# Where the eight sample rows get their scan projections and their convolution

## What is computed

```python
h = rmsnorm(x, norm_mix_w)
q, k, v, z, xbc, dt_raw = split_in(h @ w_in)      # 1024 | 256 | 256 | 1024 | 1536 | 16 columns
o_att = sink_attention(q, cache_k + k, cache_v + v, ...)
xpad = concat([state_conv, xbc], axis=1)          # 3 old rows, 1 new
new_conv = xpad[:, -3:]
xbc = silu(causal_dwconv(xpad, conv_w) + conv_b)  # 4 taps, 1536 channels
dt = softplus(dt_raw + dt_bias)
y, new_ssm = ssd_recurrent(xs, dt, A, bs, cs, ssm)
x += concat(rmsnorm(o_att), rmsnorm((y + d_skip * xs) * silu(z))) @ w_out
```

## Time and profile before

| | |
|---|---|
| time, median of 3 runs | 4440.74 us (4435.55 to 4442.08) |
| time of the profiled execution | 4443.82 us |
| its span in the trace | 4442.0 us |
| PE busy | 3836.0 us, 86% of the span |
| VectorE busy | 2496.3 us, 56% |
| ScalarE busy | 1308.7 us, 29% |
| GpSimd busy | 1353.9 us, 30% |

### The profile page before, as it was taken

How to read it: one execution, slowest core, us unless ns; L and a number is a source line. 1 busy time by engine, 2 the same in 40 slices (tenths; PEclk the granted TensorE clock), 3 DMA queues, 4 the chain that set the end, 5 groups by cost and what they waited for, 6 DMA issues and landing times.

```text
span 4442.0 us, 41911 instructions
## 1 busy us (share of the span) xinstructions
PE 3836.0 (86%) x11597; PEld 1976.8 (45%) x11597; DVE 2496.3 (56%) x5472; ACT 1308.7 (29%) x3879; POOL 1353.9 (30%) x1243
## 2 busy tenths in 40 slices
PE   8998789896888699998889999889999888877776
PEld 4555244553452345543445543345554344433332
DVE  2333256653412577654577754587755468766664
ACT  2333023331010132342233342233324233333332
POOL 0000033330000233443433434433344333334443
PEclk9997799997897899999999999999999999999999
DMA  6000000003604599999999999999999999999997
GB/s 211 29 28 33 33 15 19 19 9 122 266 15 165 231 418 418 419 418 421 420 402 405 418 420 420 421 394 410 412 420 412 421 419 400 418 418 397 419 421 298
DMA packets 227231, 1316.62 MB, mean 296 GB/s; under 512 B 27225, under 2 KB 43518, under 8 KB 93345
## 3 DMA queue, kind: packets, MB, share of 16 engines
q0 software_dynamic: 148608, 1082.20, 58.9%
q1 hardware_dynamic: 77272, 232.15, 14.0%
q10 hardware_dynamic: 1152, 0.00, 0.0%
HBM read 1283.65 MB, written 32.68 MB: 296 GB/s over the span
## 4 chain that ended last, share of the span: by engine, by line
DMA 26%; PE 26%; DVE 7%; issue 3%; ACT 2%; DVEq 1%; ACTq 0%; POOL 0%; POOLq 0%
DMA ex_ring<-in_expert_uv,ex_idx 25%; PE psum L2758 17%; DVE ex_ring L3143 4%; PE psum L2787 4%; PE psum L2736 3%; ACT ex_diag L2939 1%; PE psum L2806 1%; PE psum L2831 0%; ACT ex_weight L2934 0%; DMA ex_ring<-in_expert_uv,ex_idxT 0%; PE psum L2848 0%; POOL ex_ring L2678 0%; DMA pair_p<-scratch_mixed 0%; DVE ex_top_at L3038 0%; ACT ex_dots L2930 0%
## 5 line engine op out<-in xcount | busy, mean ns | idle before, releaser
L2758 PE MATMUL psum<-ex_ring,ex_diag 128*128 128x512 f32 x4096 | 1919.8, 613 | 332.1 <-ACT ex_diag L2939 308.9
L3143 DVE CUSTOM_DVE_ANT_0 ex_ring<-ex_ring,ex_x_rows 128x1024 f32<-128x1024 f32 x1024 | 1250.4, 1226 | 825.1 <-DMA ex_ring<-in_expert_uv,ex_idx 752.6
L2678 POOL DMA_INDIRECT ex_ring<-in_expert_uv,ex_idx x1024 | 1137.1, 1110 | 1754.8 <-PE psum L2758 1556.4
L2758 PEld LDWEIGHTS psum<-ex_ring,ex_diag 128*128 128x128 f32 x4096 | 772.6, 195 | 1303.1 <-issue 850.9
L2930 ACT ACTIVATE ex_dots<-ex_dots 128x2 f32<-128x2 f32 x512 | 104.1, 203 | 1790.5 <-DVEq L3146 1790.0
L2939 ACT ACTIVATE ex_diag<-ident,ex_weight 128x128 f32<-128x128 f32 x1024 | 355.0, 394 | 36.9 <-issue 1.7
L1062 PE MATMUL psum<-w_zx,ssd_hT 128*128 128x512 f32 (+1 forms) x768 | 295.8, 542 | 21.5 <-DMA ssd_hT<-scratch_hT 20.8
L2736 PE MATMUL psum<-ex_xT,ex_chunk 128*128 128x256 f32 (+1 forms) x1280 | 278.2, 362 | 4.2 <-ACT ex_sub L2915 2.9
L2736 PEld LDWEIGHTS psum<-ex_xT,ex_chunk 128*128 128x128 f32 x1280 | 230.3, 192 | 98.3 <-issue 77.4
L2934 ACT ACTIVATE ex_weight<-ex_gates,ex_dots 128x1 f32<-128x1 f32 x1024 | 245.8, 287 | 36.2 <-issue 1.1
L1062 PEld LDWEIGHTS psum<-w_zx,ssd_hT 128*128 128x128 f32 x768 | 137.6, 193 | 176.3 <-issue 154.6
(11 more groups left out here) (455 smaller groups left out, 3708.6 us busy)
## 6 DMA issues: line engine op xcount, KB each, us to landing
ex_chunk<-in_route_wq SPq DMA_DIRECT2D x80, 512.0 KB, 7.9
ex_chunk<-in_w_out SPq DMA_DIRECT2D x48, 512.0 KB, 9.5
ex_ring<-in_expert_uv,ex_idx POOLq DMA_INDIRECT x1024, 20.3
ex_chunk<-in_read_wq SPq DMA_DIRECT2D x24, 512.0 KB, 8.0
ex_chunk<-in_w_mo SPq DMA_DIRECT2D x24, 512.0 KB, 7.9
w_zx<-in_w_in SPq DMA_DIRECT2D x1, 10304.0 KB, 35.6
w_out<-in_w_out SPq DMA_DIRECT2D x2, 4096.0 KB
w_out<-in_cache_mem_k SPq DMA_DIRECT2D x8, 1024.0 KB, 13.3
```

Source lines behind the costliest of these rows:

```text
L2678: nc.gpsimd.indirect_dma_start(out=ring[:, n % RING, :], out_offset=None, in_=io["expert_uv"], in_offset=bass.IndirectOffsetOnAxis(ap=idx[ ...
L2758: ins = nc.tensor.matmul(psum[c][:], diag[:, q % 3, s, :], ring[:, n % RING, D + c * BANK:D + (c + 1) * BANK], start=(n % SLOTS == 0), sto ...
L3143: nc.vector.tensor_tensor_reduce(ring[:, n % RING, 0:D], ring[:, n % RING, 0:D], x_rows[:, tile % 3, :], 1.0, 0.0, ALU.mult, ALU.add, dots ...
```

## The change

The stage `ssd_sample_inputs` is gone. Its projections stand in `attention_sample`: the first of the six blocks behind the scores and ahead of the turning of p, the five others behind the value products. ScalarE takes all six blocks from PSUM into a buffer `own_zx` that lives until the scan's end: two takes behind its exponentials, four behind the square of `o`; z's two blocks with SiLU. The value products go to other PSUM banks, and the norm of `o` gets a buffer of its own. The convolution, softplus and their loads and stores stand in `ssd_prompt`: VectorE runs `own_step` ahead of its first turn, ScalarE its three activations ahead of its first turn (and so ahead of the first `load_rstd`), SyncE its loads and stores between those of the head. The products of the taps are made in place, in the buffers of the weights.

```diff
-def attention_sample(nc, io, psum, shared, w_qkv):
+def attention_sample(nc, io, psum, shared, w_qkv, w_zx, own_zx):
...
+        zx_chunks = ((1024, 4), (1536, 6), (2048, 7), (2560, 0), (0, 4), (512, 6))
+        value_banks = (1, 2, 3, 5)
...
         def _(pe):
+            def project_zx(i):
+                cols, bank = zx_cols(i), zx_chunks[i][1]
+                if i >= 4:
+                    pe.wait_ge(zx_taken, i - 3)
+                for b in range(DB):
+                    ins = nc.tensor.matmul(psum[bank][0:DEC, 0:cols.stop - cols.start], hT[:, b, :], w_zx[:, b, cols],
+                                           start=(b == 0), stop=(b == DB - 1))
+                ins.then_inc(zx_projected, 1)
...
             ins.then_inc(scored, 1)
+            project_zx(0)
             pe.wait_ge(p_ready, 1)
...
             ins.then_inc(valued, 1)
+            for i in range(1, 6):
+                project_zx(i)
...
         def _(act):
+            def take_zx(i):
+                cols, bank = zx_cols(i), zx_chunks[i][1]
+                act.wait_ge(zx_projected, i + 1)
+                nc.scalar.activation(own_zx[:, cols], psum[bank][0:DEC, 0:cols.stop - cols.start],
+                                     ACT.Silu if i >= 4 else ACT.Copy, scale=rstd[:]).then_inc(zx_taken, 1)
...
             nc.scalar.activation(esink[:], esink[:], ACT.Exp).then_inc(esum, 1)
+            take_zx(0)
+            take_zx(1)
             act.wait_ge(o_in, 16)
             nc.scalar.activation(junk[:], o[:], ACT.Square, accum_out=ms[:]).then_inc(oms_ready, 1)
+            for i in range(2, 6):
+                take_zx(i)
+            act.wait_ge(zx_taken, 6)
...
-def ssd_prompt(nc, io, psum, shared, w_zx):
+def ssd_prompt(nc, io, psum, shared, w_zx, own_zx):
...
             sp.dma_start(skip[:], io["d_skip"].broadcast_to([P, NH])).then_inc(loaded, 16)
+            sp.dma_start(past[:], io["state_conv"]).then_inc(own_loaded, 16)
+            for k in range(CONV - 1):
+                sp.dma_start(weights[:, k, :], io["conv_w"][k:k + 1, :].broadcast_to([DEC, CONV_DIM])).then_inc(own_loaded, 16)
+            sp.dma_start(io["s_conv"][:, 0:CONV - 2, :], io["state_conv"][:, 1:CONV - 1, :]).then_inc(own_stored, 16)
+            sp.dma_start(io["s_conv"][:, CONV - 2, :], own_x).then_inc(own_stored, 16)
+            sp.dma_start(io["gates"], own_zx[:, 0:D]).then_inc(own_stored, 16)
+            sp.wait_ge(own_weighed, 1)
+            sp.dma_start(last_weight, io["conv_w"][CONV - 1:CONV, :].broadcast_to([DEC, CONV_DIM])).then_inc(own_last_in, 16)
+            sp.dma_start(own_bias, io["conv_b"].broadcast_to([DEC, CONV_DIM])).then_inc(own_last_in, 16)
             load(1)
+            sp.wait_ge(own_dt_ready, 1)
+            sp.dma_start(io["dts"], own_raw[:]).then_inc(own_stored, 16)
+            sp.wait_ge(own_cv_ready, 1)
+            sp.dma_start(io["rows2"], cv_own[:, 0:D]).then_inc(own_stored, 16)
+            sp.dma_start(io["bcs"], cv_own[:, D:CONV_DIM]).then_inc(own_stored, 16)
             with sp.Fori(0, TILES - 2) as t:
...
             nc.scalar.activation(rate[:], rate[:], ACT.Exp).then_inc(rates_ready, 1)
+            act.wait_ge(own_neg_ready, 1)
+            nc.scalar.activation(own_e[:], own_neg[:], ACT.Exp).then_inc(own_e_ready, 1)
+            act.wait_ge(own_u_ready, 1)
+            nc.scalar.activation(own_neg[:], own_u[:], ACT.Ln).then_inc(own_log_ready, 1)
+            act.wait_ge(own_convolved, 1)
+            nc.scalar.activation(cv_own, cv_own, ACT.Silu).then_inc(own_cv_ready, 1)
             turn(None, 0)
...
+            def own_step():
+                nc.vector.tensor_tensor(own_raw[:], own_dt, dt_bias[0:DEC, :], ALU.add)
+                dve.drain()
+                nc.vector.scalar_tensor_tensor(own_neg[:], own_raw[:], -1.0, own_raw[:], ALU.mult, ALU.min)
+                nc.vector.tensor_scalar(own_raw[:], own_raw[:], 0.0, None, ALU.max)
+                dve.drain()
+                dve.sem_inc(own_neg_ready, 1)
+                dve.wait_ge(own_loaded, 16 * CONV)
+                for k in range(CONV - 1):
+                    nc.vector.tensor_tensor(weights[:, k, :], weights[:, k, :], past[:, k, :], ALU.mult)
+                dve.drain()
+                dve.sem_inc(own_weighed, 1)
+                dve.wait_ge(own_e_ready, 1)
+                nc.vector.tensor_scalar(own_u[:], own_e[:], 1.0, None, ALU.add).then_inc(own_u_ready, 1)
+                nc.vector.tensor_tensor(cv_own, cv_own, weights[:, 1, :], ALU.add)
...
+                nc.vector.tensor_tensor(cv_own, cv_own, weights[:, 2, :], ALU.add)
...
+                dve.wait_ge(own_last_in, 32)
+                nc.vector.tensor_tensor(last_weight, last_weight, own_x, ALU.mult)
+                dve.drain()
+                nc.vector.tensor_tensor(cv_own, cv_own, last_weight, ALU.add)
+                dve.wait_ge(own_log_ready, 1)
+                nc.vector.tensor_tensor(own_raw[:], own_raw[:], own_neg[:], ALU.add).then_inc(own_dt_ready, 1)
+                dve.drain()
+                nc.vector.tensor_tensor(cv_own, cv_own, own_bias, ALU.add).then_inc(own_convolved, 1)
...
+            own_step()
             turn(None, 0)
...
-def ssd_sample_inputs(nc, io, psum, shared, w_zx):
...
-                attention_sample(nc, io, psum, shared, w_qkv)
-            ssd_prompt(nc, io, psum, shared, w_zx)
-            ssd_sample_inputs(nc, io, psum, shared, w_zx)
+                attention_sample(nc, io, psum, shared, w_qkv, w_zx, own_zx)
+            ssd_prompt(nc, io, psum, shared, w_zx, own_zx)
```

More of the change, by code:

```diff
@@ L713, in attention_sample @@
         half = sb("sat_half", [DEC, 1])
+        orstd = sb("sat_orstd", [DEC, 1])
         hT = sb("sat_hT", [P, DB, DEC])
@@ L741, in attention_sample, with zx_cols @@
         stored = sem("sat_stored")
+        zx_projected, zx_taken = sem("sat_zx_projected"), sem("sat_zx_taken")
+        zx_chunks = ((1024, 4), (1536, 6), (2048, 7), (2560, 0), (0, 4), (512, 6))
+        value_banks = (1, 2, 3, 5)
+        def zx_cols(i):
+            col = zx_chunks[i][0]
+            return slice(col, min(col + BANK, IN_COLS - 1536))
         block = stage.block()
@@ L807, in _ @@
             for b in range(DEC):
-                out = psum[4 + b // 2][0:HEADS, (b % 2) * 256:(b % 2 + 1) * 256]
+                out = psum[value_banks[b // 2]][0:HEADS, (b % 2) * 256:(b % 2 + 1) * 256]
                 nc.tensor.matmul(out, pT[:, b, :], v_cache[:, b, :], start=True, stop=False)
@@ L834, in _ @@
             nc.gpsimd.memset(half[:], -0.5)
-            for ready, done in ((ms_ready, rstd_ready), (oms_ready, orstd_ready)):
+            for root, ready, done in ((rstd, ms_ready, rstd_ready), (orstd, oms_ready, orstd_ready)):
                 pool.wait_ge(ready, 1)
@@ L838, in _ @@
                 pool.drain()
-                nc.gpsimd.tensor_tensor(rstd[:], ms[:], half[:], ALU.pow).then_inc(done, 1)
+                nc.gpsimd.tensor_tensor(root[:], ms[:], half[:], ALU.pow).then_inc(done, 1)
         @block.vector
@@ L896, in _ @@
             for b in range(DEC):
[L897 removed]
+                nc.vector.tensor_tensor(wide[:, b], psum[value_banks[b // 2]][0:HEADS, (b % 2) * 256:(b % 2 + 1) * 256].rearrange("p (g d) -> p g d", g=KV),
                                         shared["head_mask"][:, :, None].broadcast_to([HEADS, KV, HD]), ALU.mult)
@@ L901, in _ @@
             dve.wait_ge(orstd_ready, 1)
-            nc.vector.tensor_scalar(o[:], o[:], rstd[:], None, ALU.mult).then_inc(out_ready, 1)
-def ssd_prompt(nc, io, psum, shared, w_zx):
+            nc.vector.tensor_scalar(o[:], o[:], orstd[:], None, ALU.mult).then_inc(out_ready, 1)
+def ssd_prompt(nc, io, psum, shared, w_zx, own_zx):
     ident, tri, ones, conv = (shared[k] for k in ("ident", "tri", "ones", "conv"))
@@ L944, in ssd_prompt @@
         state = sb("ssd_state", [P, D])
+        own_x, own_dt = own_zx[:, D:D + CONV_DIM], own_zx[:, D + CONV_DIM:D + CONV_DIM + NH]
+        past = sb("own_past", [DEC, CONV - 1, CONV_DIM])
+        weights = sb("own_weights", [DEC, CONV - 1, CONV_DIM])
+        last_weight, own_bias, cv_own = past[:, 0, :], past[:, 1, :], weights[:, 0, :]
+        own_raw, own_neg, own_e, own_u, own_err, own_inv = (sb("own_" + n, [DEC, NH]) for n in ("raw", "neg", "e", "u", "err", "inv"))
         def by_head(ap):
@@ L982, in ssd_prompt @@
         loaded, rates_ready = sem("ssd_loaded"), sem("ssd_rates_ready")
+        own_loaded, own_weighed, own_last_in = sem("own_loaded"), sem("own_weighed"), sem("own_last_in")
+        own_neg_ready, own_e_ready, own_u_ready, own_log_ready, own_dt_ready = (
+            sem("own_" + n) for n in ("neg_ready", "e_ready", "u_ready", "log_ready", "dt_ready"))
+        own_convolved, own_cv_ready, own_stored = sem("own_convolved"), sem("own_cv_ready"), sem("own_stored")
         state_turned, state_copied, tail_out = sem("ssd_state_turned"), sem("ssd_state_copied"), sem("ssd_tail_out")
@@ L1040, in _ @@
             sp.wait_ge(tail_out, 32)
```

(19 more changed lines are left out.)

113 lines of the change are left out of this document (removed).

## The result

The changed kernel takes 4401.97 us (median of 4 runs, 4398.42 to 4407.74), beside 4438.15 for the kernel before on the same chip (4 runs): a ratio of 0.9913, with an interval of 0.9900 to 0.9927. Two later comparisons gave 0.9924 (0.9909 to 0.9938, 6 runs) and 0.9925 (0.9911 to 0.9939, 5 runs). In microseconds the medians lie 36.2, 33.6 and 29.6 apart.

The account below looks back on a forecast made before the run. Stages before the experts stand in a row behind barriers, so a stage's length adds in full. -45.27 + 14.4 + 1.2 = -29.7 us takes the profiled 4443.82 to 4414.1, or 4411.0 against the runs' median; range 4399 to 4420.

Parts of the forecast that it names:

- The removed stage, -45.27: Stage between the scan and the memory's keys: all 45.27 us, one barrier among them, would go.
- Block 0 at no cost: Sample's attention: block 0 fits PE's idle time between scores and p's turning, 474.7 to 481.6; cost 0.
- The value products, seven passes warm: Sample's attention: 7 passes at the upper clock, then 25 x 0.48 us; end at 498.9 for 500.8, a gain of 1.9.
- Blocks 1 to 5: Sample's attention, behind the value products: 28.0 us plus 2.2 cold beginning, PE ending at 529.1; the stage grows by 14.4.
- The scan's head, +1.2: Convolution moved to the scan's start: x turned at 548.2 for 547.01, 1.2 us later, carried to the stage's end.
- only then does ScalarE issue the first load of rstd: Scan's head: load issued after ScalarE's SiLU of 1.48 us ends at 544.3, in at about 546.5.
- Tables: Scan's head: ScalarE's table loads fall into its waits; the one ahead of Exp ends at 548.5, before its input at about 549.3.
- The total: Whole kernel: -45.27 + 14.4 + 1.2 = -29.7 us, forecast 4411.0; chance 0.60.
- warm throughout: Rival, sample's attention: clock stays up through gaps and value products; stage +6.2, in all -37.9, 4402.8 us; chance 0.24.
- the head held up: Rival, scan's head: load rounds take 10 and 6 us, the chain ends 5 us later; -24.7, 4416 us; chance 0.09.
- the pairs of expert tiles: Rival, expert stage: all four pairs come out 8 us longer, +32.1 against -29.7; +2.4, 4443 us; chance 0.05.
- the rival of cold blocks: Rival, sample's attention: clock never rises for blocks 1 to 5, 56 us; stage +42, in all -2, 4439 us; chance 0.02.

Follow-up runs that it names:

- block0_late: Changed kernel with the first block of projection issued behind the value products, not ahead of p's turn: sample's attention 101.56 us, whole time 4417.04 us (one run).
- fill_all: Three products of block 1 in the gaps, two of block 0 ahead of the scores, first rstd load earlier, against the changed kernel: 4394.06 us, 0.9895 of the kernel before.
- fill_gaps: Changed kernel with three products of block 1 put into the two gaps ahead of the value products: sample's attention 83.37 us; 4396.14 us in a later comparison.

## Why the prediction was right, step by step

- **The removed stage, -45.27.** Right: no stage stands between the scan and the memory's keys, and nothing of it came back behind. The stages up to the experts came out 1.2 us shorter on the mean, in every profile without the stage; the sum had no term for that.
- **Block 0 at no cost.** Right, and worth more than nothing: without it in that place the stage is 7.8 us longer (`block0_late`).
- **The value products, seven passes warm.** Right in size: three products of two passes and a part of the fourth, and their end 60.1 us behind the stage's first transfer for 60.25 forecast (498.9 - 438.65). The ground given, that the gaps ahead let the clock fall, is borne out by `fill_gaps`, though `fill_all` held it across a gap of 1.88 us with one product behind. That it is just seven was the luck of three profiles of five; in two it was none, at 1.5 us more.
- **Blocks 1 to 5.** Right: 30.48 us for 28.0 + 2.2, the cold beginning being 2.5. PE's end comes 518.53 - 427.94 = 90.6 us into the stage, forecast 529.1 - 438.65 = 90.45, and the stage grew by 14.42 for 14.4.
- **The scan's head, +1.2.** Mis-sized: +0.3 at x's turn (+0.6 on the mean of three profiles) and none at the SiLU behind. Of its steps the loads were too short: the four were in 8.9 us after the first one's issue (532.46 - 523.52), not 7. VectorE's chain was taken 0.9 too long (547.43 - 532.46 = 15.0 for 15.9). What failed is the step "only then does ScalarE issue the first load of rstd": the queue issued it at the SiLU's start, at 547.43, not behind its 1.48 us. The kernel before had shown as much: its load went out at 523.10, and the activation in front of it had begun at 523.09. With that and the shorter chain the load landed 0.7 us earlier than forecast, counted from the scan's first transfer, late loads and all. Nor was the delay carried on: the copies behind the turning waited for the small operations on dt, and began 1.55 us behind it before (548.56 - 547.01) and 1.08 in after (552.11 - 551.03).
- **Tables.** The load ahead of Exp ran from 550.31 to 551.59, its input came at 551.74. The 2.66 us of the Trainium skill's page "ScalarE: Activation LUTs", section "What ACT_TABLE_LOAD costs", would have ended at 552.97; this case's rows show 1.28 for the load and no drain on that path.
- **The total.** The sum was -29.7; with the head at 0 it is -30.9, and the stages of two runs of after and three of before give -33.7. Of the other 2.8, 1.2 are the stages up to the experts; the rest lies in differences of the scan and the experts, each within its own spread. The medians of three comparisons, -36.2, -33.6 and -29.6, have intervals some 12 us wide: the second and third hold either sum, the first (-32.4 to -44.4) only the -33.7. The total alone would not have decided between the forecast and a rival: 4401.97 lies 0.8 from the 4402.8 of "warm throughout", which did not happen, and 9.0 from the forecast, while the later medians of after are 4407.19 and 4409.83. It is the stage's +14.4, in place of that rival's +6.2, that decides.

The rival "warm throughout" was false for this kernel and true for its mechanism: filled gaps kept the clock and gave 10.4 us where it had put 8.2 (2.6 of the 10.4 are the three products' own length, which left the tail). The other rivals left no mark: the blocks lost 2.5 us to a cold beginning and then ran warm, the head held up no more than the forecast allowed, the pairs of expert tiles took 721.4 and 729.3. The 42 us of the rival of cold blocks are 40 by the sum's own terms (14.4 + 56 - 30.2), which its chance of 0.02 makes no matter.

## What to carry to other kernels

A stage of its own between barriers is added to the time in full, so price its removal by its length, and the moved work by the idle time it finds: 6.9 us of projection cost nothing in a wait of PE. The 30.5 us behind the last value product cost 14.4, since they ran beside VectorE's path to the store: from the last value product to the next stage it is 33.6 us for 17.2 before, and that product ends 2.0 us earlier in its stage. When work is moved into an engine's waits, cut it to the waits' sizes, small ones too: three products in gaps of 1.9 and 0.8 us were worth 10.4 us here, 2.6 of their own length and the rest because TensorE stayed at its upper clock behind them. And before a few microseconds are put down to an edit, compare each untouched stage in several runs of both kernels.

## What was unexpected of the hardware

- The prompt's attention, the same instructions in each kernel, took 427.8 to 443.0 us in fourteen profiles; the granted clock over the whole stage was 0.91 in the shortest and 0.87 in the longest (a tile took 47.89 us at 1.00 and 53.46 at 0.87).
- The clock's fall in one schedule came at places up to some 3 us apart in different runs: in two profiles 0.5 us into the turning of p, in three 1.7 to 1.9 us into the value products.
- Value products of 256 columns, half of them contracting over 8 rows, kept the clock at 1.00 for 8.5 us but never raised it from 0.50 in 15.5 us; the scores, of 129 columns over 128 rows, were at 0.50 for 3.5 us and then back at 1.00 (`fill_gaps`, 470.0 to 473.5):

```profile
470.00:471.00 1.00, 1.00 (x7) 0.72 (x6) 0.00 (x0) 0.00 (x0) 0.00 (x0) 0.53 0.00 0
...
473.00:474.00 1.00, 1.00 (x9) 0.75 (x7) 0.00 (x0) 0.00 (x0) 0.00 (x0) 0.77 0.00 0
474.00:475.00 1.00, 1.00 (x10) 0.78 (x9) 0.00 (x0) 0.00 (x0) 0.00 (x0) 1.00 0.00 0
```
